# Low halves of split weights: a VectorE subtraction, or a DMA that adds the weights onto a negated copy

## The reference, cut to what matters

```python
h = x                                            # (1, 512, 2048) float32
z = einsum("bsd,de->bse", h, w_in) + b_in        # w_in is 2048 x 14352
glu_val, glu_gate, gate_c, q, k, v, f_logit, gate_a = split(z)
y_conv = conformer_conv(glu_val, glu_gate, ...)  # u = val*sigmoid(gate), 31 taps, layer norm, silu
y_conv = y_conv * silu(gate_c)
y_attn = forgetting_attention(q, k, v, f_logit)  # 16 heads of 128, causal, decay by cumsum of log f
y_attn = y_attn * silu(gate_a)
sub = einsum("bse,ed->bsd", concat(y_conv, y_attn), w_out) + b_out
out = layer_norm(DN_ALPHA * h + sub, g_post, b_post)
```

## Time and profile before

| | |
|---|---|
| median of the runs | 1766.29 us |
| span of the profiled execution | 1763.0 us |
| PE busy | 1733.5 us, 98% |
| DVE busy | 1071.8 us, 61% |
| ACT busy | 539.6 us, 31% |
| POOL busy | 215.4 us, 12% |
| DMA moved | 178.09 MB, 101 GB/s over the span |

### The profile page before, as it was taken

One profiled execution on the slowest core, in us unless ns is written; L12 is line 12 of the kernel. 1 busy time (PEld: TensorE's weight loads), 2 busy tenths in 40 slices (PEclk: granted clock), 3 DMA queues, 4 the chain that ended last, 5 costly groups with the idle time before them and its releaser, 6 DMA issues. The chain is left out here.

```text
span 1763.0 us, 21898 instructions
## 1 busy us (share of the span) xinstructions
PE 1733.5 (98%) x7644; PEld 1400.0 (79%) x7644; DVE 1071.8 (61%) x1669; ACT 539.6 (31%) x791; POOL 215.4 (12%) x176
## 2 busy tenths in 40 slices
PE   7999999999999999999999999999999999999997
PEld 5888888888888888888888888888688877788885
DVE  4356757667586575765857657577754565344347
ACT  4323223222232232223223232232544432222240
POOL 0120101201012010110111101100200044000000
PEclk8999999999999999999999999999999999999999
DMA  5333342333323433333333333333233333332232
GB/s 157 109 110 87 95 110 71 110 97 94 100 73 108 105 91 96 77 104 110 95 92 77 108 100 95 98 83 86 70 108 96 119 131 132 124 115 95 95 120 96
DMA packets 259691, 178.09 MB, mean 101 GB/s; under 512 B 8193, under 2 KB 246945, under 8 KB 258737
## 3 DMA queue, kind: packets, MB, share of 16 engines
q1 hardware_dynamic: 258656, 170.39, 33.6%
q0 software_dynamic: 1008, 7.34, 1.2%
HBM read 173.48 MB, written 4.23 MB: 101 GB/s over the span
## 5 line engine op out<-in xcount | busy, mean ns | idle before, releaser
L635 PE MATMUL ps<-xh,wh 128*128 128x512 f32 x1792 | 716.4, 400 | 0.7 <-DVE wl L876 0.7
L636 PE MATMUL ps<-xl,wh 128*128 128x512 f32 x1792 | 711.9, 397 | 0.0
L637 PE MATMUL ps<-xh,wl 128*128 128x512 f32 x1792 | 711.5, 397 | 0.0
L876 DVE TENSOR_TENSOR wl<-raw,wh 128x1024 fp32r<-128x1024 f32 x280 | 370.3, 1324 | 391.0 <-ACT wh L388 387.1
L635 PEld LDWEIGHTS ps<-xh,wh 128*128 128x128 f32 x1792 | 338.8, 189 | 81.5 <-DVE wl L876 0.8
L637 PEld LDWEIGHTS ps<-xh,wl 128*128 128x128 f32 x1792 | 338.4, 189 | 81.8
L636 PEld LDWEIGHTS ps<-xl,wh 128*128 128x128 f32 x1792 | 338.9, 189 | 80.1 <-issue 0.5
L388 ACT ACTIVATE wh<-raw 128x1024 fp32r<-128x1024 f32 x280 | 288.2, 1054 | 297.0 <-PE ps L637 221.8
L921 DVE SCALAR_TENSOR_TENSOR y<-u,taps,y 128x512 f32 (+1 forms) x240 | 193.6, 807 | 0.0
L921 DVE SCALAR_TENSOR_TENSOR odd<-u,taps,odd 128x512 f32<-128x512 f32 x224 | 186.6, 833 | 0.0
L635 PE MATMUL ps<-wh,yh 128*128 128x512 f32 x464 | 183.0, 394 | 3.1 <-DVE yl L1162 3.1
(11 more groups left out here) (167 smaller groups left out, 1068.3 us busy)
## 6 DMA issues: line engine op xcount, KB each, us to landing
raw<-in_w_in_dram SPq DMA_DIRECT2D x224, 512.0 KB, 3.7
raw<-in_w_out_dram SPq DMA_DIRECT2D x64, 512.0 KB, 3.6
probs<-forget_sums_dram SPq DMA_DIRECT2D x16, 256.0 KB, 7.4
res<-in_x_dram POOLq DMA_DIRECT2D x4, 1024.0 KB, 5.3
out_dram<-res SPq DMA_DIRECT2D x8, 512.0 KB, 2.7
probs<-forget_sums_dram SPq DMA_DIRECT2D x16, 192.0 KB, 6.2
probs<-forget_sums_dram SPq DMA_DIRECT2D x16, 128.0 KB, 4.8
y<-in_x_dram SPq DMA_DIRECT2D x2, 768.0 KB, 9.0
```

What stands on the lines that cost most here:

```text
L635: nc.tensor.matmul(o, ah, bh, start=start, stop=False, skip_group_check=True)
L636: nc.tensor.matmul(o, ah, bl, start=False, stop=False, skip_group_check=True)
L637: return nc.tensor.matmul(o, al, bh, start=False, stop=True, skip_group_check=True)
L876: vec.tensor_tensor(wl[:, 2 * par + h, :], raw[:, h, :], wh[:, 2 * par + h, :], ALU.subtract) \
```

## The change: what it does

In the head loop (tiles K to GLU of every head, Q of heads 1 to 15, and the first GATE_C tile: 96 tiles, 192 halves) the low half is made in another way. ACT writes the high half as before, and then a second time rounded and negated into the low slot (`negate`: `wl = -raw`, rounded to fp32r). Then POOL issues a DMA that reads the same 512 KB of `w_in` out of HBM again and adds them onto `wl` in SBUF (`add_raw`, `accum_op=ALU.add`). What is left in `wl` is `raw - wh`. PE waits for that DMA (`acc_done`, one semaphore for each of the four slots) and not for `low_done`. SP may load the next half into `raw` when the negated copy has been written (`neg_done`). The 192 subtractions of DVE are gone. The forget tile, the first Q tile and all that follows the first GATE_C tile are as before, with counts shifted by `A_UNITS`. POOL's loop over the heads is written out.

The core of the diff:

```diff
+A0, A1 = T_BODY + 1, T_GATE
+A_UNITS = 2 * (A1 + 1 - A0)
...
+            def raw_free(t, h, before):
+                if before == "split":
+                    sp.wait_ge(low_done, 2 * t + h - 1)
+                elif before == "negated":
+                    sp.wait_ge(neg_done, 2 * t + (h - 1 - 2 * A0))
+                else:
+                    sp.wait_ge(low_done, 2 * t + (h - 1 - A_UNITS))
...
+            def add_raw(t, kind, i):
+                for h in range(2):
+                    pool.wait_ge(neg_done, 2 * (t - A0) + h + 1)
+                    src = w_in[D // 2 * h:D // 2 * (h + 1), ds(col_of(kind, i), P)]
+                    nc.gpsimd.dma_start(wl[:, 2 * (t % 2) + h, :].rearrange("p (k c) -> p k c", k=HALF),
+                                        src.rearrange("(k p) c -> p k c", p=P), accum_op=ALU.add) \
+                      .then_inc(acc_done[2 * (t % 2) + h], 16)
+            for i in range(HEADS):
+                t = i * PER_HEAD + T_BODY
+                add_raw(t + 1, K, i)
+                add_raw(t + 2, V, i)
                 bias(i)
-                add_conv(i - 1)
+                add_raw(t + 3, GATE_A, i)
+                add_raw(t + 4, VAL, i)
+                add_raw(t + 5, GLU, i)
+                if i:
+                    add_conv(i - 1)
+                if i < HEADS - 1:
+                    add_raw(t + 6, Q, i + 1)
+                else:
+                    add_raw(t + 6, GATE_C, 0)
...
+            def negate(par, h):
+                nc.scalar.activation(wl[:, 2 * par + h, :], raw[:, h, :], ACT.Copy, scale=-1.0).then_inc(neg_done, 1)
...
                 high(t + 1, 0, 0)
+                negate(0, 0)
                 high(t + 1, 0, 1)
+                negate(0, 1)
...
-                half(t + 3, 0, 0)
+                half(t + 3, 0, 0, added=i * 3 + 2)
...
-                low(t + 1, 0, 0)
                 taps_of(0, 0)
-                low(t + 1, 0, 1)
                 taps_of(0, 1)
```

More of the change, by code:

```diff
@@ L196, in build @@
         high_done, low_done, half_done = sem("high_done"), sem("low_done"), sem("half_done")
+        neg_done, acc_done = sem("neg_done"), [sem(f"acc_done{n}") for n in range(4)]
         f_act, f_vec, f_pad = sem("f_act"), sem("f_vec"), sem("f_pad")
@@ L224, in _, with load_in @@
         def _(sp):
-            def load_in(t, col, second_first=False):
+            def raw_free(t, h, before):
[5 more added lines that the diff above has]
+                    sp.wait_ge(low_done, 2 * t + (h - 1 - A_UNITS))
+            def load_in(t, col, second_first=False, before="negated"):
                 for h in (1, 0) if second_first else (0, 1):
                     if not (second_first and h == 0):
-                        sp.wait_ge(low_done, 2 * t + h - 1)
+                        raw_free(t, h, before)
                     src = w_in[D // 2 * h:D // 2 * (h + 1), ds(col, P)]
@@ L236, in load_out @@
                 for h in range(2):
-                    sp.wait_ge(low_done, 2 * t + h - 1)
+                    raw_free(t, h, "late")
                     sp.dma_start(raw[:, h, :], w_out[ds(row + P * h, P), half_cols * 1024:half_cols * 1024 + 1024]) \
@@ L273, in body @@
                     if s + 1 < PER_HEAD:
-                        load_in(t + 1, col_of(BODY_KINDS[s + 1], 0) + i * P, BODY_KINDS[s + 1] == VAL)
+                        load_in(t + 1, col_of(BODY_KINDS[s + 1], 0) + i * P, BODY_KINDS[s + 1] == VAL,
+                                "split" if first and s == 0 else "negated")
                     if s == 1 and first:
@@ L294, in _ @@
                 load_in(T_BODY + i * PER_HEAD + s, col_of(BODY_KINDS[s], i))
-            with nc.sync.Fori(0, HEADS) as j:
-                load_in(j + T_GATE, col_of(GATE_C, 0) + j * P)
+            for j in range(2):
+                load_in(j + T_GATE, col_of(GATE_C, j))
+            with nc.sync.Fori(2, HEADS) as j:
+                load_in(j + T_GATE, col_of(GATE_C, 0) + j * P, before="late")
             for p in range(2):
@@ L454, in body @@
                 high(t + 2, 1, 0)
+                negate(1, 0)
                 high(t + 2, 1, 1)
+                negate(1, 1)
                 tile_done(t + 1)
@@ L637, in mm3, with half @@
                 return nc.tensor.matmul(o, al, bh, start=False, stop=True, skip_group_check=True)
-            def half(t, par, h, beside=None):
-                pe.wait_ge(low_done, 2 * t + (h + 1))
+            def half(t, par, h, beside=None, added=None):
+                if added is not None:
+                    pe.wait_ge(acc_done[2 * par + h], added * 16)
+                elif isinstance(t, int) and t < A0:
+                    pe.wait_ge(low_done, 2 * t + (h + 1))
+                else:
+                    pe.wait_ge(low_done, 2 * t + (h + 1 - A_UNITS))
                 for k in range(HALF):
@@ L694, in body @@
                     pe.wait_ge(val_read, i)
-                half(t, 1, 0)
-                half(t, 1, 1)
+                half(t, 1, 0, added=None if i0 else i * 3)
+                half(t, 1, 1, added=None if i0 else i * 3)
                 if i0:
@@ L704, in body @@
                     pe.wait_ge(glu_tanh, i)
-                half(t + 1, 0, 0)
-                half(t + 1, 0, 1)
+                half(t + 1, 0, 0, added=i * 3 + 1)
+                half(t + 1, 0, 1, added=i * 3 + 1)
                 pe.wait_ge(qk_low, i * 2 + 1)
-                half(t + 2, 1, 0)
+                half(t + 2, 1, 0, added=i * 3 + 1)
                 pe.wait_ge(qk_low, i * 2 + 2)
@@ L715, in body @@
                     mm3(o, qh[:, m], ql[:, m], kh[:, c], kl[:, c], True).then_inc(scores_done, 1)
-                half(t + 2, 1, 1)
-                half(t + 3, 0, 0)
+                half(t + 2, 1, 1, added=i * 3 + 1)
+                half(t + 3, 0, 0, added=i * 3 + 2)
                 pe.wait_ge(vt_done, i + 1)
@@ L725, in body @@
                 last.then_inc(v_turned, 1)
-                half(t + 3, 0, 1)
-                half(t + 4, 1, 0)
+                half(t + 3, 0, 1, added=i * 3 + 2)
+                half(t + 4, 1, 0, added=i * 3 + 2)
                 pe.wait_ge(probs_done, i * NT + NT)
@@ L735, in body @@
                     last.then_inc(p_turned, 1)
-                half(t + 4, 1, 1)
+                half(t + 4, 1, 1, added=i * 3 + 2)
                 pe.wait_ge(gate_read, i * 2 + 2)
-                half(t + 5, 0, 0)
+                half(t + 5, 0, 0, added=i * 3 + 3)
                 pe.wait_ge(ptl_done, i * NT + NT)
@@ L747, in body @@
                 last.then_inc(pv_done, 1)
-                half(t + 5, 0, 1)
+                half(t + 5, 0, 1, added=i * 3 + 3)
             body(0, True)
@@ L761, in _ @@
                     pe.wait_ge(z_read, 2 * j - 2)
-                half(T_GATE + j, (j + 1) % 2, 0)
-                half(T_GATE + j, (j + 1) % 2, 1)
+                added = (T_GATE // 2) if j == 0 else None
+                half(T_GATE + j, (j + 1) % 2, 0, added=added)
+                half(T_GATE + j, (j + 1) % 2, 1, added=added)
                 if j == 2:
@@ L1024, in body @@
                 taps_of(4, 1)
-                low(t + 6, 1, 0)
-                low(t + 6, 1, 1)
                 dve.wait_ge(pv_done, i + 1)
```

16 lines of the change are left out of this document (2 added, 14 removed).

## The result

The changed kernel takes 1905.5 us (median of two runs, 1904.04 to 1906.96) against 1766.29: a ratio of 1.0795, 95% interval 1.0778 to 1.0813. It is 8% slower. The forecast was 1855 us, slower, in a range of 1762 to 2200.

What follows compares the result with a forecast made beforehand. TensorE, busy 98%, was taken to bound the kernel. Additions landing late cost 5.6 us per head (Q 4.5, V 0.8, VAL 0.3), 90 us over 16 heads: 1763.0 + 90, plus 3.3 around the span, about 1855 us; range 1762 to 2200.

Steps and rivals of the forecast that it cites:

- the tile that decides: Q's first half in the head loop: 5.7 us from DMA issue to landing, the tightest window.
- VectorE's relief is worth 0: Head loop: dropping 192 subtractions of 1.32 us, 254 us of VectorE beside PE work, gains no time.
- ACT's copies cost nothing: Head loop: 192 negated copies of 1.05 us cost PE nothing by themselves; they only move the DMA's start.
- Issue G = 2.0 us: Time POOL takes to issue one accumulating DMA of 1024 pieces; low end 0.6, high end 4.8 us.
- Moving S = 3.9 us: Time to move one 512 KB addition, two 512-byte reads per piece; low end 1.93, high end 14 us.
- The rest, 1.4 us: What remains of a raw load's 3.7 us from issue to landing after 0.37 of issue and 1.93 of moving.
- Sharing with the raw load, 9.2 us: Addition's 7.3 us plus 1.9 because SP's next raw load shares the 16 DMA engines.
- The windows: DMA time before PE needs each first half: VAL 8.9, GLU 9.0, Q 5.7, K 8.5, V 8.4, GATE_A 10.4 us.
- POOL's bias work: 8.7 us on POOL ahead of GATE_A's additions: shrinks GATE_A's window from 10.4 to about 8.7 us, without lateness.
- DMA work 72 us in a head of 78: nearly full: Per head 12 x 5.8 us plus some 2.4 for bias rows, leaving no room below the estimate's faults.
- The engine-bound rival: Additions moving in over 4 us each make the 16 DMA engines set the pace: 2140 us at 5.9; chance 0.32.
- The rule from the skill: A GpSimd DMA takes 2.0 us plus bytes at 436 GB/s; by it every window holds and time is unchanged.

## Why the prediction was right, point by point

Direction, cause and the tile that decides were as forecast, and the time lies in the range. That the terms come out so close is in part luck: errors in the landing cancel, and so do those of the windows, while one term of 50 us is missing.

- *TensorE bounds the kernel, VectorE's relief is worth 0, ACT's copies cost nothing.* Right, to 0.1% (the run without the DMAs). ACT's copies took 1.05 us each, as forecast.
- *Issue G = 2.0 us.* It is 1.55. *Moving S = 3.9 us.* By rate it is 2.9 alone (183 GB/s). I had doubled 1.93 us, which was itself a packet time; a stretch of raw loads alone, 825 to 827 us in the kernel before, shows 320 GB/s, 1.6 us, under a share of 108%:

```profile
DMA packets 1242, 0.64 MB, mean 320 GB/s; under 512 B 18, under 2 KB 1234, under 8 KB 1242
...
q1 hardware_dynamic: 1242, 0.64, 108.0%
```

  The term was too large by 1.0, and the idea behind it, that the old value has to be read as well, fits the rates (adding moves 0.59 of what copying does) but is argued, not shown. *The rest, 1.4 us*, was too small: nearly alone, in the run with small raw loads, the landing is 7.3 us, which is 1.55 + 2.9 and 2.8 more. (These 2.8 are a difference and not measured; part of them may be a second half that queues behind the first, as the shortest landing of that run is 6.3.) Three terms were off and their sum, 7.3, was met: that is luck.
- *Sharing with the raw load, 9.2 us.* Landing 8.9; the raw loads' cut showed 1.6 us for my 1.9.
- *The windows.* Q 4.5 us late per head: 3.7 (8.5 from issue to PE). V 0.8: 0.67. VAL 0.3: about 1.6. Here a step failed: I charged the shared engines to the addition and not to the raw load, which grew from 3.7 to 7.8 us. VAL's two raw halves are issued together, beside both additions of GATE_A, and ACT had to wait for them. In all 5.6 per head were forecast, 90 us; 92.5 were measured, again because Q's term was too large and VAL's too small. POOL's bias work did not delay anything that PE waited for.
- *"DMA work 72 us in a head of 78: nearly full."* The trace after agrees, with a share of 96.8% from 400 to 1200 us, and both are misread. The rates leave room: by an estimate from them, 12 x (2.9 + 1.7) us is 55 of a head of 81. The engine-bound rival did not come. That waits move from tile to tile (Q's to VAL, VAL's to Q) fits transfers that are close together in time better than full engines, but it is argued and not shown.
- *What was not in the sum at all:* the granted clock. The prediction put the price of a wait at the wait itself. 48.5 of 142.2 us by the mean clock, 50.7 by PE's busy time. Put onto the 1855 afterwards, it gives about 1904.
- *The rule from the skill.* Section "Anatomy of one DMA — SWDGE (gpsimd) path" of DMA: Bandwidth & Descriptors (the Trainium skill) gave an estimate of 3.2 us for 512 KB. No landing of such a DMA came near: 4.3 us at least for a copy, 6.1 at least for an addition (in the run with VAL's small raw loads; 6.2 in the change). The traces decide, and they say that this estimate is too low for a transfer in 1024 pieces of 512 bytes with other loads beside it. Where the Trainium skill (Collectives: The Full Stack, Stop ④ — SDMA + CCE: where bytes move and the add happens) calls the add itself free, no run here tells the add from the second read: together they brought 309 GB/s down to 183.

No version here beats the kernel before: PE is busy for 98% of its span, and none of the edits takes a matmul away.

## What to carry to other kernels

Before moving work from an idle engine to a DMA, lay the windows side by side: from the release of the step to the first instruction that needs it, tile by tile, and against the whole latency, issue and landing. The engine taken off had 5 us to spare and was worth nothing; its replacement, with 8.9 us, missed one window of 5.7 and touched those of 8.4 and 8.9, and that decided. And a wait of TensorE has a second price: at 1.0 us the clock took next to nothing, at 2.8 and 3.8 us half as much again, and in one execution as much again.

## What was not expected of the hardware

- An addition onto SBUF costs issue time on GpSimd by its pieces: 1.55 us for 1024 pieces of 512 bytes, 1.28 for 512, 0.87 for 128 of 4 KB; a copy of 1024 pieces 0.88.
- Adding runs at 183 GB/s with pieces of 512 bytes and at 211 with pieces of 4 KB, in a stretch without long gaps; copying with pieces of 512 bytes, on the same queue, at 309.
- The DMA share of the profile sums packets that overlap. For the software queue it read 211.9% in a stretch of copies at 309 GB/s and 144.9% in one of additions at 183, so it is no measure of how full the engines are.
- Fifteen pauses of TensorE of 3.8 us, a head apart, took the mean clock from 0.994 to 0.979, with nothing else changed.
